# A float32 transformer pair on one core: activation rows at a pitch of 513 words, weight slots at a pitch of 1028 words

## The reference

```python
proj = (n @ w_in[l]).astype(f32)                       # 1024 x 7712
h = h + (merged @ w_out[l].astype(f32)).astype(h.dtype)
u = rmsnorm(h, norm_ffn_g[l]) @ ffn_w1[l]              # 1024 x 4096
h = h + (jnp.square(jax.nn.relu(u)) @ ffn_w2[l]).astype(h.dtype)
...
proj = h @ w_in                                        # second block, per layer
u = h @ w_up                                           # 1024 x 5632
return (jax.nn.gelu(a, approximate=False) * b) @ w_down
```

## Time and profile before

| | |
|---|---|
| median of 3 runs | 2912.06 us (2911.98 to 2912.39) |
| span of the profiled execution | 2909.9 us |
| TensorE (PE) busy | 2892.3 us, 99% |
| VectorE (DVE), GpSimd (POOL), ScalarE (ACT) busy | 1572.7, 1584.3, 1103.5 us |
| granted TensorE clock, mean | 0.998 |
| 16 DMA engines | 111 GB/s in the mean |

### The profile page before, as it was taken

How to read it: one execution, slowest core, us unless ns; L and a number is a source line. 1 busy time by engine, 2 the same in 40 slices (tenths; PEclk the granted TensorE clock), 3 DMA queues, 4 the chain that set the end, 5 groups by cost and what they waited for, 6 DMA issues and landing times.

```text
span 2909.9 us, 49401 instructions
## 1 busy us (share of the span) xinstructions
PE 2892.3 (99%) x19658; PEld 2423.8 (83%) x19658; DVE 1572.7 (54%) x2227; ACT 1103.5 (38%) x1673; POOL 1584.3 (54%) x1912
## 2 busy tenths in 40 slices
PE   9999999999999999999999999999999999999998
PEld 7877777788888888888888898888898888988887
DVE  5467877524556666775334265445763441473635
ACT  4454434333443322443433343233443342342323
POOL 6432233355646666677444557565584444565654
PEclk9999999999999999999999999999999999999999
DMA  5211111332426777533222323232333222232232
GB/s 173 94 45 41 42 55 45 97 141 95 130 82 217 252 273 254 179 113 126 85 89 73 95 87 113 87 109 87 106 124 115 77 88 87 87 102 94 94 102 73
DMA packets 92292, 322.21 MB, mean 111 GB/s; under 512 B 10144, under 2 KB 14368, under 8 KB 91808
## 3 DMA queue, kind: packets, MB, share of 16 engines
q1 hardware_dynamic: 84544, 302.39, 31.7%
q10 hardware_dynamic: 7520, 16.67, 1.7%
HBM read 315.09 MB, written 3.93 MB: 110 GB/s over the span
## 4 chain that ended last, share of the span: by engine, by line
PE 98%; issue 1%; DVE 1%; POOL 1%; DMA 0%; ACT 0%; POOLq 0%; SPq 0%; ACTq 0%; DVEq 0%
PE bank L906 25%; PE bank L910 25%; PE bank L907 25%; PE bank L1254 2%; PE bank L899 2%; PE bank L901 2%; PE bank L900 2%; PE bank L1265 2%; PE bank L1273 1%; PE bank L934 1%; PE bank L936 1%; PE bank L935 1%; PE bank L958 1%; PE bank L960 1%; PE bank L1785 1%
## 5 line engine op out<-in xcount | busy, mean ns | idle before, releaser
L837 POOL TENSOR_TENSOR w_lo<-w_raw,w_hi 128x256 fp32r<-128x256 f32 x1736 | 1419.2, 852 | 986.9 <-ACT w_hi L1862 980.5
L906 PE MATMUL bank<-act,w_hi 128*128 128x512 f32 (+1 forms) x3464 | 1312.7, 379 | 4.7 <-POOL w_lo L837 2.6
L910 PE MATMUL bank<-act,w_lo 128*128 128x512 f32 (+1 forms) x3464 | 1292.4, 373 | 0.0
L907 PE MATMUL bank<-act,w_hi 128*128 128x512 f32 (+1 forms) x3464 | 1291.4, 373 | 0.0
L906 PEld LDWEIGHTS bank<-act,w_hi 128*128 128x128 f32 x3464 | 652.9, 188 | 126.1 <-issue 8.3
L910 PEld LDWEIGHTS bank<-act,w_lo 128*128 128x128 f32 x3464 | 652.6, 188 | 115.2
L907 PEld LDWEIGHTS bank<-act,w_hi 128*128 128x128 f32 x3464 | 653.4, 189 | 106.7
L1862 ACT CAST w_hi<-w_raw 128x1024 fp32r<-128x1024 f32 (+1 forms) x438 | 454.4, 1043 | 345.1 <-DMA w_raw<-in_weights 163.6
L1870 ACT ACTIVATE arena<-bank 128x512 f32<-128x512 f32 (+1 forms) x177 | 104.3, 593 | 418.2 <-PE bank L910 401.6
L855 POOL TENSOR_TENSOR stats<-stats,exponent 128x8 f32<-128x8 f32 (+2 forms) x38 | 46.6, 1226 | 302.5 <-DVE stats L2914 150.0
L2600 DVE TENSOR_TENSOR act<-tmp,act 128x512 fp32r<-128x512 f32 (+1 forms) x140 | 121.2, 866 | 77.3 <-ACT act L1889 72.7
(11 more groups left out here) (359 smaller groups left out, 3087.4 us busy)
## 6 DMA issues: line engine op xcount, KB each, us to landing
w_raw<-in_weights SPq DMA_DIRECT2D x471, 512.0 KB, 3.5
arena<-in_ada SPq DMA_DIRECT2D x96, 512.0 KB, 5.0
arena<-in_strips ACTq DMA_DIRECT2D x8, 448.0 KB, 3.7
arena<-in_x ACTq DMA_DIRECT2D x1, 2048.0 KB, 10.9
y_scratch<-tmp ACTq DMA_DIRECT2D x7, 256.0 KB, 2.0
arena<-y_scratch ACTq DMA_DIRECT2D x1, 1792.0 KB, 8.1
arena<-in_dft ACTq DMA_DIRECT2D x2, 777.5 KB, 4.2
arena<-in_x SPq DMA_DIRECT2D x3, 512.0 KB, 7.4
```

The costliest lines, as they stand in the source:

```text
L837: ins = nc.gpsimd.tensor_tensor(w_lo[:, k, cols], weights_of(u)[:, cols], w_hi[:, k, cols].bitcast(F32), ALU.subtract)
L906: nc.tensor.matmul(o, wh, xh, start=first, stop=False)
L907: nc.tensor.matmul(o, wh, xl, start=False, stop=False)
L910: mm = nc.tensor.matmul(o, wl, xh, start=False, stop=last)
```

## The change

The rows of `act1` and `act2` get a pitch of 513 words: each row keeps its 512 words, and one word stays empty behind it. The slots of `w_hi` and `w_lo` get a pitch of 1028 words, with four empty words behind each. `w_raw` stays as it is. Buffers that lie in the bytes of `act2` are moved to the new rows, and all that is allocated behind `w_hi` begins later. No instruction is added, removed or put elsewhere, and no operand changes its shape.

```diff
+SLOT_PAD, PITCH = 4, S + 1
...
-        w_hi = sb("w_hi", [P, RING, UNIT], F32R)
-        w_lo = sb("w_lo", [P, RING, UNIT], F32R)
+        w_hi = sb("w_hi", [P, RING, UNIT + SLOT_PAD], F32R)[:, :, 0:UNIT]
+        w_lo = sb("w_lo", [P, RING, UNIT + SLOT_PAD], F32R)[:, :, 0:UNIT]
...
-        with nc.sbuf_tensor("arena2", [P, 2 * KT * S], F32) as arena2:
+        with nc.sbuf_tensor("arena2", [P, 2 * KT * PITCH], F32) as arena2:
             pass
-        acts = {"A2": sb("act2", [P, 2, KT, S], F32R), "A1": sb("act1", [P, 2, KT, S], F32R)}
+        acts = {name: sb(buf, [P, 2, KT, PITCH], F32R)[:, :, :, 0:S] for name, buf in (("A2", "act2"), ("A1", "act1"))}
...
-        free_at[0] = 5 * KT * S // 4 + 3 * S
+        free_at[0] = (KT + 5) * PITCH
...
-        SCS = (take(2, 1280), arena2[:, 4 * KT * S // 4:4 * KT * S // 4 + 2560].rearrange("p (e k) -> p e k", k=1280))
+        SCS = (take(2, 1280), arena2[:, KT * PITCH:KT * PITCH + 2560].rearrange("p (e k) -> p e k", k=1280))
```

## The result

The changed kernel takes 2961.47 us (median of four runs, 2961.22 to 2961.55), the kernel before 2912.02 us beside it (2911.98 to 2912.39). The ratio is 1.017, with an interval of 1.0157 to 1.0182: 49.5 us slower, where 39.6 were forecast. The profiled span is 2959.2 us, 49.3 more than before, and the mean granted clock 0.999. All lines behind the new constant are one higher: L907, L908 and L911 are the L906, L907 and L910 of before, and L838, L1863, L2601, L3591 and L1890 follow in the same way.

What follows compares the result with a forecast made beforehand. PE's matmul pace was taken to bound the kernel, busy 2892.3 of 2909.9 us. +43.6 - 4.8 + 0.8 = +39.6 us gave 2951.7 us, forecast alone 2943 to 2967, whole range 2870 to 2976.

Steps and rivals of the forecast that it cites:

- Steps (1) and (2): Wide projection matmuls: padded rows and slots put operands out of step, 226.7 to 232.0 ns on 8219 steps, +43.6 us.
- two regimes: PE's matmuls: in step at 226.7 ns wide, 119.9 narrow with congruent operands; otherwise out of step, 231 to 233 and 117.
- Step (3): Narrow matmuls, 1731 steps: 119.9 to 117.1 ns as in the spectrum, -4.8 us, or 0 if they gain nothing.
- 384-column steps: 157 token-major steps in step: +0.8 us at the wide ones' 5.3 ns, or 0.
- Step (4): Rows not beginning on a 16-byte line: no price put on it; an estimate of about +10 us was set aside.
- Steps (5) and (6): Other engines unaffected, set at 0; cross attention, retention and spectrum matmuls also 0, with +/-0.8 us possible.
- The rival that is faster: Wide projection steps: new phases are good ones, 223.5 ns or less, giving 2881 or 2859 us; chance 0.22.
- The rival of no change: PE's steps: the extra 13.3 ns is the engine's own, or matmuls fall in step along moving phases; 2912 us, chance 0.12.
- rows 5 and 6: Profile evidence: L1626 and nine projection matmuls after it, 231.7 and 231.1 ns each; six retention matmuls, 233.3.
- The much slower rival: Wide steps: worse phases or dearer starts off the line, at 237 ns +85 us, 2992 us; chance 0.08.
- The signs to look for: After trace: varying steps, about 862 matmuls per 200 us window, narrow near 117, other engines' fastest durations kept, PE idle near 18 us.

Runs made afterwards that it cites:

- bursts: Kernel before, with repeated matmuls behind its end, each series at one address pattern; at distance 0, 226.7 ns a step at 512 columns, 119.8 at 256.
- 200 random patterns: Kernel before, with series of 36 wide matmuls behind it, rows and weights at randomly drawn places; 232.8 ns a step in the mean, fastest settled 227.8.
- bursts of 30: Kernel before, with 30 matmuls per distance behind it, each series entered through one odd matmul, five entries wide, three narrow; mean 232.9 ns wide, 119.2 narrow.
- bursts of 48: Kernel before, with 48 matmuls behind it at each of 64 distances and both widths, plus tile patterns; wide steps from 226.7 to near 240.0 ns.

## Why the prediction held, and where it was off

*What bounds.* Right. PE's idle time is 18.4 us after 17.6, and the whole difference lies in the steps.

*Steps (1) and (2), rows and slots.* The mechanism held as far as it says that the pace hangs on where the row stands against the weights, with the congruent place the best for wide steps. That there are just two regimes did not hold: whole kernels have wide steps of 229.2 ns at 16 words, 233.2 at 8 and 239.5 at 5. The size was a little low. The prediction took 232.0 ns from three rows of cross attention and retention, and the changed kernel has 232.8. On 8219 steps that is 0.8 x 8219 = 6.6 us, the largest part of the 9.9 that the sum was short of. One of the three, 231.1, isn't of that kind: those nine projection steps have congruent operands and are on their way back into step. The other two, 231.7 and 233.3, have a mean of 232.5, which would have given 47.7 us. And the rows were samples of something that runs from 226.7 to 240.0; that they gave nearly the mean of all places (232.9) was partly luck. The step called the places congruent modulo 512 bytes. It is 256, as the gap of that size shows, with 884 matmuls in the window; this changes nothing for the pitches of 513 and 1028 words, but by the prediction's rule that gap would have cost all that the change does. The step also laid stress on places that differ between successive operands; a constant distance of 32 bytes costs just as much.

*Step (3), narrow matmuls.* The sign was right, the term was mis-sized: -4.8 us forecast, about -1.2 measured. The 117.1 ns came from the spectrum, one place, and the mean over places is 119.2, near the 119.8 of before. That is 3.6 us of the shortfall. The 384-column steps were put at +0.8 us and measured 1 ns each, 0.2 us.

*Step (4), rows off a line of 16 bytes.* No price was put on it, and in the sum that was near enough: rows alone, with three in four off the line, cost 43 us, slots alone, with none, 44. As a statement on the hardware it was too simple. Some odd places are as fast as any (7, 15, 39 and 63 words in bursts), yet distances of 1 modulo 4 words take 236.5 ns and those of 3 modulo 4 take 229.1, with 232.6 for whole lines. Rows of a 513-word pitch visit all four, so that much of it may cancel; this is a reading that no run separates. The estimate from the Trainium skill (SBUF — State Buffer, "SBUF: two separate sides"), a price on each line crossed, would make all off-line rows slower alike; the 226.7 at 7 words speaks against that.

*Steps (5) and (6).* Right: the durations of the four lines on VectorE, ScalarE and GpSimd stand as they were, and cross attention, retention and the spectrum moved the sum by about nothing. Of the reads at words 8 and 9 the prediction took the fastest; their medians are 751 and 1107 ns, and 752 and 1107 in the changed kernel. So the 1107 doesn't come from the change, but no run shows what it comes from, and the evidence that an off-line row costs VectorE nothing is L2601.

*The rival that is faster* falls. It decided where the wide mean falls under 226.7 ns, and not one of 64 distances, five entries each, nor of 200 random patterns goes there (the least, 226.6 in a few bursts of 30, is the pace of distance 0 to the 0.1 ns that can be read). Its argument, that the 10.2 ns on top of the spectrum's columns could belong to the place and not to the width, is half right: at 256 columns the best places pay 113.3 - 106.7 = 6.6 ns, at 512 no place tried pays less than 13.3.

*The rival of no change* falls as well. Its sentence from the Trainium skill (SBUF — State Buffer, "Who interferes with whom"), by which PE's two ports are independent and PE never waits, gave that no address matters. That does not hold for these steps: 226.7, 233.3 and 240.0 ns for the same matmul by the place of its operands alone. Whether it is at the ports that the two operands meet no run shows. That rows 5 and 6 were slow because their operands had just been written is excluded by the bursts, whose operands nobody writes and which still take up to 240.0. That matmuls might fall in step along the moving place is excluded by the 861 of the window.

*The much slower rival* had a real mechanism, a dearer place. The change doesn't stay in one, since its rows and slots pass through all; 5 words for both buffers do, and cost 111.6 us.

*The signs to look for.* The window was to hold about 862 and holds 861. Steps vary and don't settle, and the other engines' fastest durations stay. Narrow steps near 117 did not come; they are at 119.1. The forecast's own range of 2943 to 2967 us held the 2961.47.

## What to carry to other kernels

For a PE-bound kernel of float32r matmuls whose weights change every time, lay out the streamed rows and the weights at the same place modulo 256 bytes: pitches that are multiples of 256 bytes, and starts that lie multiples of 256 bytes apart (the starts themselves needn't be such multiples: in the kernel before both operands begin 128 bytes past one). A pad against imagined bank conflicts, or one small buffer put in between, costs in the mean over all places about 2.7% of each 512-column step (232.9 against 226.7 ns), without any wait showing in the profile. With 256 columns the place hardly matters in the mean (119.2 against 119.8 ns). What shows it is the distance of successive starts, or the number of matmuls in a window of projections. Don't read one place off a line as all such places, nor a burst as a kernel: 63 words held 226.7 from every way into a burst, and whole tiles there took 230.2.

## What the hardware showed that I had not expected

- A gap of 32 bytes between two buffers costs 50.3 us of 2912 (2962.32 us), and one of 256 bytes nothing (2912.07).
- The paces often fall on a raster. The pace that a burst holds is often 226.7, 230.0, 233.3 or 240.0 ns wide and 113.3, 116.7, 120.0 or 123.3 narrow; at 2.4 GHz, the level that was granted, these are 544, 552, 560 and 576 periods, and 272, 280, 288 and 296. In the bursts of 48, every settled step at 11 words is 230 ns and every one at 5 words 240. Most other distances repeat steps of different lengths, whose mean may fall on the raster (24 words, 230, 232 and 238 ns) or beside it (1 word, 236.6; 3 words, 228.9). What makes the raster no run here shows.
- The same distance can hold different paces, by what ran before it (236.7, 233.4 and 226.7 ns at 60 words), while at distance 0 it is 226.7 from every entry tried.
- The best place for 512 columns (0 words, 226.7 ns) is not the best for 256 (119.8). 28 words have 113.3 there, once settled, in every burst; 4, 16 and 48 words have it in some and 117.8 or 118.6 in others.
- Moving both operands by one word, distance unchanged, takes the step from 226.7 to 237.9 ns. Moving both by 8, 16 or 24 words does nothing.
